# GpSimd scatters an item's gates in bursts of four indirect transfers, each burst after the landing of the last

## What is computed

```python
v1, i1 = lax.top_k(s1, 16)                 # per token and head, over 128 keys
v2, i2 = lax.top_k(s2, 16)
cand = v1[..., :, None] + v2[..., None, :]
best, pos = lax.top_k(cand, 16)            # 16 experts of 16384 per token and head
expert = take_along_axis(i1 * 128 + i2, pos)
gate = softmax(best)
a  = x . w_down[expert]
y  = (gelu(a) * gate) @ w_up[expert]       # summed over 8 heads x 16 picks
```

## Time and profile before

| | us |
|---|---|
| median of 3 executions | 2907.55 |
| lowest and highest | 2896.77, 2939.85 |
| span of the profiled execution | 2911.8 |
| GpSimd: first scatter issued | 1213.4 |
| GpSimd: first load of gates issued | 1686.5 |
| TensorE: first product of the up stage | 1701.2 |

### The profile page before, as it was taken

The page is one execution under the profiler, slowest core; times in us unless marked ns, Lnnn a source line. Parts: engine busy times, 40 slices in busy tenths (PEclk is TensorE's granted clock), DMA queues, the critical chain, the costliest instruction groups (busy, mean ns, idle before and its releaser), DMA issues.

```text
span 2911.8 us, 38726 instructions
## 1 busy us (share of the span) xinstructions
PE 2606.5 (90%) x12676; PEld 2026.3 (70%) x12676; DVE 2035.1 (70%) x4029; ACT 1279.4 (44%) x2143; POOL 1134.8 (39%) x1481
## 2 busy tenths in 40 slices
PE   8998899999989979888999999999897888887776
PEld 7886688778878867778898978788775433333332
DVE  7776477687767754666797956677685777766675
ACT  5555455555545544434454545554452222222221
POOL 4431044344335410255586733333101444444442
PEclk9999899999999988888999999999998999999999
DMA  9984299899869974434554689999756999999997
GB/s 362 367 303 144 100 349 380 318 354 372 313 255 372 346 277 170 130 112 135 159 181 150 196 307 386 379 390 390 243 192 236 412 419 421 413 419 420 407 417 302
DMA packets 217528, 873.30 MB, mean 300 GB/s; under 512 B 38272, under 2 KB 38400, under 8 KB 183744
## 3 DMA queue, kind: packets, MB, share of 16 engines
q0 software_dynamic: 118496, 511.47, 45.0%
q1 hardware_dynamic: 98768, 359.38, 34.7%
q10 hardware_dynamic: 144, 1.05, 0.1%
HBM read 786.70 MB, written 152.17 MB: 322 GB/s over the span
## 4 chain that ended last, share of the span: by engine, by line
PE 66%; DMA 19%; DVE 9%; issue 3%; ACT 3%; POOL 1%; another core or an unknown queue 0%; SPq 0%; DVEq 0%; ACTq 0%; POOLq 0%
PE ps L1674 13%; PE ps L1676 13%; PE ps L1675 13%; DMA arena<-both_rows,arena 12%; PE ps L1746 12%; PE ps L1748 6%; DMA both_rows<-in_stream 5%; PE ps L2083 5%; DVE arena L1586 2%; DMA raw<-in_stream 1%; PE ps L2049 1%; DVE w_lo L1024 1%; PE ps L1849 1%; PE ps L1718 1%; PE ps L1800 1%
## 5 line engine op out<-in xcount | busy, mean ns | idle before, releaser
L1024 DVE TENSOR_TENSOR w_lo<-raw,w_hi 128x1024 fp32r<-128x1024 f32 x665 | 811.3, 1223 | 390.4 <-ACT w_hi L632 355.8
L632 ACT ACTIVATE w_hi<-raw 128x1024 fp32r<-128x1024 f32 x665 | 702.5, 1058 | 505.2 <-DMA raw<-in_stream 346.0
L2083 PE MATMUL ps<-arena 128*128 128x512 f32 x1024 | 478.1, 613 | 136.3 <-ACT arena L822 136.1
L1746 PE MATMUL ps<-act_both,w_hi 128*128 128x512 f32 x1408 | 505.8, 401 | 3.0 <-DVE act_both L1052 3.0
L2083 PEld LDWEIGHTS ps<-arena 128*128 128x128 f32 x1024 | 190.1, 193 | 413.5 <-ACT arena L822 216.1
L1586 DVE SCALAR_TENSOR_TENSOR arena<-arena 128x1024 f32<-128x1024 f32 x256 | 313.6, 1225 | 194.2 <-DMA arena<-both_rows,arena 191.9
L561 POOL DMA_INDIRECT arena<-both_rows,arena x256 | 294.9, 1152 | 367.9 <-PE ps L2083 334.1
L500 POOL DMA_DIRECT2D both_rows<-arena x512 | 280.1, 554 | 391.5 <-DVE arena L1107 382.0
L1674 PE MATMUL ps<-w_hi,act_both 128*128 128x512 f32 (+1 forms) x990 | 386.8, 391 | 23.5 <-DVE w_lo L1024 6.7
L1748 PE MATMUL ps<-act_both,w_lo 128*128 128x256 f32 x1408 | 397.0, 282 | 0.0
L1675 PE MATMUL ps<-w_lo,act_both 128*128 128x512 f32 (+1 forms) x990 | 384.0, 388 | 0.0
(11 more groups left out here) (255 smaller groups left out, 3449.9 us busy)
## 6 DMA issues: line engine op xcount, KB each, us to landing
raw<-in_stream SPq DMA_DIRECT2D x675, 512.0 KB, 3.2
arena<-in_stream POOLq DMA_DIRECT2D x128, 512.0 KB, 9.2
both_rows<-arena POOLq DMA_DIRECT2D x512, 128.0 KB, 5.9
both_rows<-in_stream POOLq DMA_DIRECT2D x128, 512.0 KB, 6.8
gate_cells<-hot POOLq DMA_DIRECT2D x32, 512.0 KB, 17.9
hot<-gate_cells POOLq DMA_DIRECT2D x128, 128.0 KB, 6.9
gate_cells<-hot POOLq DMA_INDIRECT x256
arena<-both_rows,arena POOLq DMA_INDIRECT x256, 10.8
```

The source lines that it names most:

```text
L632: act.activation(w_hi[:, u % SPLIT, :], raw[:, u % RAW, :], ACT.Copy).then_inc(hi_done, 1)
L1024: dve.tensor_tensor(w_lo[:, u % RAW, :], raw[:, u % RAW, :], w_hi[:, u % SPLIT, :].bitcast(F32), ALU.subtract).then_inc(lo_done, 1)
L1746: pe.matmul(ps[:, bank, :], high, act_both[:, :, k, :], start=k == 0, stop=k == KD - 1, skip_group_check=True)
L2083: ins = pe.matmul(ps[:, 2 * (n % 2) + half, :], diags[:, p % DIAG_RING, :], row[:, p % ROW_RING, D + 512 * half:D + 512 * half + 512], sta ...
```

## The change

Two waits of GpSimd change, and no instruction is added, removed or moved. At the start of an item it now waits until the whole item before it has landed (not the item before that), and inside an item it waits after every fourth transfer until all issued so far have landed.

```diff
@@ -56,6 +56,7 @@
 RING = 6
+BURST = 4
 HOT = 4
@@ -521,9 +522,11 @@
                 for n in range(ITEMS):
                     pool.wait_ge(value_ready, n + 1)
-                    if n >= TB:
-                        pool.wait_ge(scattered[n % TB], 16 * K16 * (n // TB))
+                    if n:
+                        pool.wait_ge(scattered[(n - 1) % TB], 16 * K16 * ((n - 1) // TB + 1))
                     for k in range(K16):
+                        if k and k % BURST == 0:
+                            pool.wait_ge(scattered[n % TB], 16 * (K16 * (n // TB) + k))
                         q = column(n) + k
                         pool.indirect_dma_start(gate_cells[:, :], bass.IndirectOffsetOnAxis(ap=cell[:, q:q + 1], axis=0),
                                                 weights[:, q:q + 1], None).then_inc(scattered[n % TB], 16)
```

## The result

The changed kernel takes 2935.14 us, the median of 20 executions (2924.66 to 2950.85). The kernel before, executed 20 times in the same series, takes 2919.7 (2894.26 to 2950.59); the 2907.55 of its first three was on the low side. The ratio is 1.0055, with a 95% interval of 1.0035 to 1.0075: slower by about 16 us. The forecast was 33.

What follows compares the result with a forecast made beforehand. The prediction took the up stage to be full and paced by GpSimd's queue, so its start decides: 38.7 us late less 6 at the seam, rounded to 33, on 2907.5 gives 2940 us; range 2912 to 2970.

Steps and rivals of the forecast that it cites:

- The direction and the place: At the end of the scatter: GpSimd reaches the gate loads 38.7 us late, making the kernel 33 us slower.
- the case of no change: Whole kernel: the measured time stays within 2% of the kernel before, chance 86%.
- The price of a wait: Between GpSimd's scatters: a landing wait replaces 0.30 us idle with 2.2 us during the down stage, 1.6 after it.
- the 2.72 us of the earlier trace: After the last scatter: the only landing gap shown, taken as upper bound of a wait, at DMA share 0.79.
- The quick end: Lower bound of a landing wait between scatters: 1.6 us, from the quickest gate load of 2.3 us.
- Items 0 to 6: the waits fill idle time and cost nothing: Early scatter: an item costs 29.5 us, weights come 33.2 us apart, so item 7 starts where it did.
- The seam: Between scatter and up stage: slack after GpSimd's first gate loads takes 6 us off the delay, between 4.3 and 10.0.
- The lower start of the clock: Start of the up stage: TensorE's clock may start lower after some 40 us idle, priced 0 to 3 us, taken as 0.
- The landing is cheap: Rival, 13%: in the scatter the landing hides in the issue, a gap is 1.3 us, kernel +3 us, 2911.
- The landing is dear: Rival, 13%: scatter waits meet weight units, 3.4 us in the down stage and 2.72 after, +76 us, 2983.
- The bursts quicken the issue: Rival, 4%: from item 7 transfers in flight slow scatters to 1.57 us; bursts restore 1.28, kernel not slower, 2907.
- theory A: Down stage, from the experiments rather than the prediction: dense scatters slow TensorE and bursts cure it.

Runs made afterwards that it cites:

- the fourth profile of before: The kernel before, unchanged, executed and profiled a fourth time: 2830.97 us, ratio 0.9993, load of gates at 1613.76.
- the scatter that was held back: Against the kernel before, GpSimd issues no scatter until the weights of all 16 items are ready: 3127.26 us, ratio 1.1035.

## Why the prediction was right, and where its sizes were not

**The direction and the place** held. The change adds waits and nothing else, GpSimd reaches the loads of gates later, and everything behind the load shifts. The time fell in the range, and the change is less than the 2% that bound the case of no change.

**The price of a wait** held in the main: 2.49 us beside the down stage and 1.53 after it, where 2.2 and 1.6 were taken. The reasoning on the 2.72 us of the earlier trace rows was half right: it was not an outlier, the mean beside a busy stream is near it. The quick end is right where nothing else moves. The fixed cost of about 2.0 us in the Trainium skill (DMA: Bandwidth & Descriptors, section Anatomy of one DMA — SWDGE (gpsimd) path), counted from the end of the issue (g = 2.3), lies between the two measured means; counted from its start (g = 1.3) it is too low for both.

**"Items 0 to 6: the waits fill idle time and cost nothing"** is the step that failed. It took VectorE's pace from the profile of before as given, 33.2 us and then 27.0 between items. In the profile after, the weights of items 7 to 15 come (1575.26 - 1372.21) / 8 = 25.4 us apart, there is no idle time between items, and all 63 waits are paid. That the load still came within 5 us of the forecast is luck, two errors that cancel: nine items were charged from 1437.87, where sixteen were paid from 1214.25. A profile of before from the second level would have shown GpSimd without idle time from item 1 to 15, and a sum on it would have charged all 63 waits.

**The seam** was priced at 6 us. From the load to the end of the span it is 2911.8 - 1686.54 = 1225.3 us before and 2935.4 - 1720.27 = 1215.1 after: it gave back 10.1, just past the upper end of 4.3 to 10.0. Of these, 7.4 lie before TensorE's first product (1701.20 - 1686.54 = 14.7 us after the load, then 1727.55 - 1720.27 = 7.3). The lower start of the clock, for whose 0 to 3 us the prediction shows no row, was rightly taken as 0: the kernel before starts the up stage at 0.50 as well. So the spans differ by 33.7 - 10.1 = 23.6 us. The prediction had everything behind the load shift by one amount; the shift is 33.7 us at the load, 26.4 at TensorE's first product of the up stage, 24.8 at the end of its last (2056.2 and 2081.0) and 23.6 at the end of the span.

**The sum against the median.** The rest is that the profile and the three executions before were low in their series: 2907.55 was the median of three, 2919.7 that of twenty. The profiled execution of before is some 6 us under that (its span of 2911.8, and about 2 us outside the span as in the one after), the one after is 2 us over its own median: 23.6 - 6 - 2 = 16 us, which is the ratio. The prediction said that the span was 4 us over the median; against twenty executions it is under it. Against the first level the forecast of 33 us is twice the result.

**The rivals.** *The landing is cheap* is refuted by 2.49 us. *The landing is dear* needed 2.9 us and a slow release in the idle stretch; single waits reach 5.3 us, the mean does not. Yet the kernel is slower by over 2% at the second level, for a reason that no rival named: not a dearer wait, but more of them uncovered. *The bursts quicken the issue* is refuted. The window of the fourth profile of before, with its scatters in one row, against that of after (above):

```profile
1213.00:1437.00 224.00, 222.79 (x1859) 222.43 (x1858) 207.12 (x570) 129.18 (x195) 176.78 (x148) 1.00 0.56 177
```

An issue takes 176.78 / 148 = 1.19 us without bursts and 127.93 / 107 = 1.20 with them, beside the same 207 us of work of VectorE. It is short where VectorE is idle, as in the scatter that was held back (203.17 / 211 = 0.96 us); but there the weight stream and the other engines are idle too, and no run parts them. The Trainium skill (GPSIMD Engine Reference, section Key points) has contention between these two; the runs agree with it, but show neither that it is VectorE's work alone nor through which interface.

**What is shown and what is open.** Shown: with a down stage lengthened to 3.6 us for a unit (30 products, 0.12 us apart), the kernel before goes to 2921.56 us and the change costs 0.7%; so a slow down stage is enough for a time like that of the first level and for a small cost of the change. Open: what slowed TensorE in the first twenty executions. In the profile of before it has gaps that end in "issue"; the same products in the page after have none (before, then after):

```profile
L1676 PE MATMUL ps<-act_both,w_lo 128*128 128x256 f32 x1192 | 348.7, 293 | 15.4 <-issue 14.6
```
```profile
L1679 PE MATMUL ps<-act_both,w_lo 128*128 128x256 f32 x1192 | 338.4, 284 | 0.0
```

The gaps of before, from 1213 to 1690:

```profile
PE ps L1676 <- issue: 14.6, 28, 0.9
PE ps L1674 <- issue: 10.8, 20, 1.0
PE ps L1675 <- issue: 8.5, 18, 1.0
```

Where these 66 gaps lie says more than their number. 51 of them begin in items 0 to 6 or just behind them: all but one come no sooner than after the item's eighth scatter, and none later than 3.1 us after the start of its last. 14 more go with item 11, which followed items 7 to 10 without a pause. The kernel after never has more than four scatters in a row. But beside items 7 to 10 and 12 to 15, which are just as dense, there is one gap in all. This fits theory A with a condition added: rows of scatters disturb TensorE only under it. That is argued, not shown: the condition never returned, so it could not be tried whether bursts cure it. Nor does the time of the changed kernel say whether its other executions in the first series were disturbed, since it hardly depends on the pace of the down stage. The later series ran on three chips, numbers 4, 11 and 13; the first series has no chip on record, so a property of its chip is not excluded.

## What to carry to other kernels

An idle gap in front of an engine is cover only if the engine that leaves it keeps its pace: before counting on it, ask how the sum comes out if the producer runs at its undisturbed speed; and take a granted clock under 1.00 in such a stage (0.87 in the slow down stage here, 1.00 in all others) as a sign that it may run faster another time. A wait for the landing of a small transfer was 1.5 us long on idle DMA engines and 2.5 beside a stream here, and where the queue has no idle time every one of them moves the total, by 1.25 to 1.84 us each; bursts of eight cost less than bursts of four, and none cost least.

## What the runs showed that was not expected

- The same kernel had two levels, 2920 and 2833 us, 3% apart, in different series, each steady within itself to 2% and 0.5%. The changed kernel had one. A ratio of two kernels can depend on the level more than on the change: 1.0055 or 1.0371.
- The changed kernel's time is nearly independent of the pace of its down stage: 2935.14 and 2937.6, and 2942.94 with 25% more products in each unit of it.
- Scatters of 128 numbers of 4 bytes start 1.56 us apart beside the down stage and 1.31 us apart when they come after it, with all other engines idle for most of that time.
